# Decode attention: values of a batch issued ahead of the third part of the next batch's keys

## What is computed

```
idx = n_buf + jnp.arange(S)[:, None] - d * jnp.arange(sub_w + 1)[None, :]
s = jnp.einsum('bshd,bsjhd->bshj', q, k_all[:, idx]) * (HEAD_DIM ** -0.5)
p = jnp.exp(s - m[..., None])
acc = jnp.einsum('bshj,bsjhd->bshd', p, v_all[:, idx].astype(jnp.float32))
```

## Time and profile before

| what | value |
|---|---|
| median of 3 runs | 3102.05 us (3100.16 to 3106.0) |
| span of the profiled execution, first to last instruction | 3097.1 us |
| PE busy | 1166.9 us, 38% |
| DVE busy | 1991.4 us, 64% |
| POOL busy | 1820.1 us, 59% |
| moved by DMA | 1010.08 MB, mean 326 GB/s |

### The profile page before, as it was taken

One profiled execution on the slowest core, in us unless ns is written; L12 is line 12 of the kernel. 1 busy time (PEld: TensorE's weight loads), 2 busy tenths in 40 slices (PEclk: granted clock), 3 DMA queues, 4 the chain that ended last, 5 costly groups with the idle time before them and its releaser, 6 DMA issues.

```text
span 3097.1 us, 22146 instructions
## 1 busy us (share of the span) xinstructions
PE 1166.9 (38%) x7904; PEld 930.8 (30%) x7904; DVE 1991.4 (64%) x2265; ACT 387.5 (13%) x499; POOL 1820.1 (59%) x901
## 2 busy tenths in 40 slices
PE   7999989999896910000000003000000000000088
PEld 6889955555686910000000001000000000000077
DVE  1016441221014499898898998988888999989922
ACT  2222233433222200000000001000000000000022
POOL 4556600000453545777967778888888878873344
PEclk9999976877897955555555556555555555555599
DMA  8878869997878778889988899999999989999844
GB/s 312 312 297 312 306 189 263 253 271 210 312 298 288 288 280 330 320 340 355 384 335 328 340 396 404 401 394 385 382 387 391 409 349 401 398 390 375 328 163 170
DMA packets 161535, 1010.08 MB, mean 326 GB/s; under 512 B 18786, under 2 KB 20258, under 8 KB 71620
## 3 DMA queue, kind: packets, MB, share of 16 engines
q0 software_dynamic: 92160, 671.13, 54.5%
q1 hardware_dynamic: 69316, 338.20, 32.5%
HBM read 1002.82 MB, written 139.01 MB: 369 GB/s over the span
## 4 chain that ended last, share of the span: by engine, by line
POOL 45%; issue 42%; DVE 6%; PE 4%; DMA 2%; POOLq 1%; DVEq 0%; ACT 0%; ACTq 0%
POOL expert_rows L457 33%; POOL w_lo L438 6%; POOL pool_token L456 5%; DVE psum L1035 4%; PE psum L1137 1%; PE psum L1139 1%; PE psum L1138 1%; DMA expert_rows<-in_peer_v,block_experts 1%; DMA expert_rows<-in_peer_u,block_experts 1%; DVE expert_rows L1031 0%; POOL gate_w_lo L438 0%; DVE expert_sums L1035 0%; POOLq L455 0%; POOLq L441 0%; PE psum L1129 0%
## 5 line engine op out<-in xcount | busy, mean ns | idle before, releaser
L1031 DVE SCALAR_TENSOR_TENSOR expert_rows<-expert_rows,x_tokens 128x2048 f32<-128x2048 f32 x320 | 727.9, 2294 | 98.5 <-DMA expert_rows<-in_peer_u,block_experts 94.9
L438 POOL TENSOR_TENSOR w_lo<-w_raw,w_hi 128x2048 fp32r<-128x2048 f32 x80 | 373.8, 4673 | 702.0 <-ACT w_hi L477 702.0
L457 POOL DMA_INDIRECT expert_rows<-in_peer_u,block_experts x320 | 612.3, 1914 | 85.5 <-issue 73.3
L1035 DVE SCALAR_TENSOR_TENSOR expert_sums<-expert_rows,block_gates,expert_sums 128x2048 f32<-128x2048 f32 x256 | 603.3, 2357 | 65.8 <-DMA expert_rows<-in_peer_v,block_experts 48.2
L457 POOL DMA_INDIRECT expert_rows<-in_peer_v,block_experts x320 | 582.7, 1821 | 84.7 <-issue 73.0
L1129 PE MATMUL psum<-identity,x_tokens 128*128 128x128 f32 (+1 forms) x144 | 24.7, 356 | 1010.1 <-DVE x_tokens L880 962.0
L456 POOL TENSOR_TENSOR pool_token<-pool_token 128x1 f32<-128x1 f32 x160 | 177.8, 1111 | 301.4 <-DVE expert_rows L1031 140.1
L1129 PEld LDWEIGHTS psum<-identity,x_tokens 128*128 128x128 f32 (+1 forms) x144 | 22.6, 204 | 1012.9 <-issue 934.2
L1360 PE MATMUL psum<-identity,ple_tokens 128*128 128x128 f32 (+1 forms) x6 | 1.5, 397 | 733.8 <-DMA ple_tokens<-in_p_sample 733.8
L1360 PEld LDWEIGHTS psum<-identity,ple_tokens 128*128 128x128 f32 (+1 forms) x6 | 1.0, 210 | 734.1 <-issue 734.0
L477 ACT ACTIVATE w_hi<-w_raw 128x2048 fp32r<-128x2048 f32 x80 | 153.2, 1916 | 442.2 <-PE psum L1139 402.6
(11 more groups left out here) (234 smaller groups left out, 2315.3 us busy)
## 6 DMA issues: line engine op xcount, KB each, us to landing
out<-in_state_attn_k SPq DMA_DIRECT2D x64, 1020.0 KB, 7.4
out<-in_state_attn_v SPq DMA_DIRECT2D x64, 1020.0 KB, 15.6
w_raw<-in_w_in SPq DMA_DIRECT2D x48, 1024.0 KB, 5.3
keys_old<-in_state_attn_k SPq DMA_DIRECT2D x16, 1536.0 KB, 17.5
values_old<-in_state_attn_v SPq DMA_DIRECT2D x8, 3072.0 KB, 17.4
keys_last<-in_state_attn_k SPq DMA_DIRECT2D x8, 2048.0 KB, 13.7
values_last<-in_state_attn_v SPq DMA_DIRECT2D x8, 2048.0 KB, 21.0
w_raw<-in_w_out SPq DMA_DIRECT2D x16, 1024.0 KB, 5.0
```

Of the source, the lines that this page charges most:

```text
L438: nc.gpsimd.tensor_tensor(l_, r_, h_.bitcast(f32), ALU.subtract).then_inc(w_lo_ready, 1)
L457: pool.indirect_dma_start(ring[:, j % NSLOT, :], None, table, bass.IndirectOffsetOnAxis(idxc[:, half, j:j + 1], 0)).then_inc(g_in[j % NSLO ...
L1031: V.scalar_tensor_tensor(out=g, in0=g, scalar=1.0, in1=x, op0=ALU.mult, op1=ALU.mult, accum_out=hblk[:, c:c + 1]).then_inc(g_free, 1)
L1035: V.scalar_tensor_tensor(out=y, in0=g, scalar=ablk[:, c:c + 1], in1=y, op0=ALU.mult, op1=ALU.add).then_inc(g_free, 1)
```

## The change

SP's loop issued K0(b+1), K1(b+1), K2(b+1), then V0(b), V1(b). Now it issues K0(b+1), K1(b+1), then V0(b), V1(b), then K2(b+1). `load_k` gets two arguments that choose parts. Each transfer keeps the wait that it had. What stands ahead of the loop and behind it stays. The loop runs six times, so K2(2) to K2(7) move. No other engine's stream changes.

```
-            def load_k(b):
+            def load_k(b, first=0, past=3):
                 bb = ds(b, 1)
-                for part, last in enumerate(K_PARTS):
+                for part, last in list(enumerate(K_PARTS))[first:past]:
...
             with sp.Fori(1, NB - 1) as b:
-                load_k(b + 1)
+                load_k(b + 1, 0, 2)
                 load_v(b)
+                load_k(b + 1, 2, 3)
```

## The result

| | before | changed |
|---|---|---|
| median of 4 runs each | 3101.11 us | 3141.69 us |
| lowest to highest | 3090.87 to 3106.0 | 3131.88 to 3150.7 |
| span of the profiled execution | 3097.1 us | 3130.1 us |

The changed kernel is slower: ratio 1.0138, 95% interval 1.01 to 1.0175. The forecast was 3140 us, range 3118 to 3160. A second, longer comparison (experiment 7) gave 1.013, 1.0096 to 1.0163.

What follows compares the result with a forecast made beforehand. The decode attention was taken to go at PE's pace. 6 x 25.2 + 5 x 21.7 = 259.7 us against 221.8, so 37.9 more on 3097.1, plus 5 for the median: 3140 us, range 3118 to 3160.

Steps and rivals of the forecast that it cites:

- No gain from the part taken away: In SP's loop, K2 no longer ahead of V0 and V1 gains nothing, since PE waits for neither there.
- When V1 lands and how much longer K2 takes: In the DMA queue, V1 lands 19.9 us behind its issue and K2 5.3 later: 25.2 us (24.3 to 28.0).
- The rest of a batch: From K2's first transpose on PE to the next issue of V1: 21.7 us in each of five batches.
- The 3.3 us for slower rests: Time added in the five stretches behind K2's first transpose, for a tail at a lower clock: 3.3 us.
- When PE asks: PE asks for K2 13.5 us behind V1's issue in batch 3, 20.3 to 21.0 otherwise; waits together 34.6 us.
- The sum: From V1(1)'s issue to K2(7)'s first transpose: 259.7 us instead of 221.8, 37.9 us more.
- A lower clock: Rival: pauses delay PE's clock rise, so five tails take 26.0 us each; 59.4 us more, 3161; chance 0.10.
- Overlap: Rival: K2 fills gaps V0 leaves in the queue and lands with V1 at 19.9 us; 3109 to 3112; chance 0.07.
- The one that ends faster: Rival: K2 lands together with V1 and PE's pause is followed by full clock; 3092 to 3096; chance 0.03.

Runs made afterwards that it cites:

- experiment 7: The changed kernel run again with no edit, for a tighter interval and a second trace; ratio to the kernel before 1.013.
- experiment 1: The kernel before run again with no edit, for a second trace; ratio 0.9987.
- experiment 8: Second trace of the changed kernel with K2 issued between V0 and V1 instead of behind both; ratio to the kernel before 1.0035.
- 10: The changed kernel with the next batch's first three groups of transposes moved ahead of PE's wait for the copied output; ratio to the kernel before 1.0108.
- experiment 9: The kernel before with the next batch's first three groups of transposes moved ahead of PE's wait for the copied output; ratio 0.9953, 3088.64 us.
- experiment 4: The changed kernel with two 1020 KB cache copies moved between V1 and K2 in each of six turns; ratio to the kernel before 1.0237.

## Why the prediction was right

**No gain from the part taken away: right.** V0 and V1 landed no earlier to any use; the one wait for values stayed (7.3 us for 7.1), and no other engine's waits for them are in the list.

**When V1 lands and how much longer K2 takes: right.** I took 19.9 and 5.3 us, 25.2 together. Six batches gave 24.3 to 25.6, in sum 149.1 for 151.2. The small difference is in the first term: V1 came at 19.1 to 19.7, 19.4 on average. K2 landed 4.9 to 5.9 us behind it, 5.4 on average, so the second term was right or a little too small.

**The rest of a batch: right.** 5 x 21.7 = 108.5 us were put down; the windows that answer to the earlier trace rows sum to 108.2, from 20.8 to 22.4 us, at clocks of 0.80 to 0.87. No batch kept the full clock behind its wait. The 3.3 us for slower rests were 3.0 against the first trace, and 5.9 against that of experiment 1. K0 and K1 were through before the next V0, as said.

**When PE asks: mis-sized for batch 3.** For it I wrote 13.5 us, from the one batch that ran at full clock, and so a wait of 11.7 us and 34.6 in all. The waits were 22.3 us and the longest 4.3. There was no batch at full clock ahead of K2, in this trace or in experiment 7. It did no harm to the sum, since the sum goes from landing to landing: what isn't waited for by a quick PE is spent by a slow one. In the window it shows as longer busy time: some 10 of the 13.2 us lie ahead of K2, and some 7 of them are batch 3 at half clock instead of full. But the name was wrong, and who looked for the loss among the waits alone would have found 22.3 of 35.5 us. Experiments 8 and 10 show the wait as I had described it, 5.64 and 5.88 us with K2 landing at 19.5, and 12 to 14 us with it landing at 25, once PE is at full clock.

**The sum.** 259.7 us were forecast for the window, and 257.3 came. The span grew by 33.0 us instead of 37.9: the window gave 35.5 but began 3.5 us earlier, and 1.0 came behind it, which is within what stages vary by from run to run (the kernel before had two spans of 3097.1 and 3114.0). The median is 40.6 us above that of before. So that 3140 misses 3141.69 by only 1.7 us is in part luck: the span came 4.9 us short of the 3135.0, and the median stands 11.6 us above it, where I had added 5. Of that distance 1.8 us lie around the span (3131.88 against 3130.1 in one execution); the rest is how quick the profiled execution was among the others. What measures the working is the window, with its 2.4 us.

**The rivals.** A lower clock (0.10): the rests took 108.2 us against the 130 it asked for. Something of it may be there, since the rests of before took 105.2 and 102.3 us, but it isn't what the loss is made of. Overlap (0.07): within one queue K2 came 4.9 to 5.9 us behind V1, and even on a queue of its own it came 22.6 to 23.2 us behind V1's issue, not 19.9. The one that ends faster needed both and had neither.

## What to carry to other kernels

Issue transfers in the order in which they are asked for, and price a move by the landing: the time that the transfers ahead of it take in the queue, from the landings of the old trace, against the time at which its reader asks; the moment of issue alone costs nothing while the landing is in time. Sum such a stage from landing to landing and not wait by wait, because an engine whose clock varies turns waits into slow work and back. And look for the reader's own gaps: a transfer that seems to have room beside a slow reader has none once the reader is quick.

## What the runs showed of the hardware

I had not expected that filling a gap of at most 1.7 us a batch would change the clock so much: from 0.74 and 0.71 in the two traces of before to 0.86 in the window, and 24 to 29 us less busy time for the same matmuls. It isn't one trace's luck: over the whole execution the twelve runs of experiment 9 have clocks of 0.665 to 0.670, and the seventeen of the kernel before beside them 0.658 to 0.664. Nor that PE can be busy without a break and stay at half clock: experiment 8 has 17.00 us of 17.00 at 0.51 in one batch and 11.00 of 11.00 at 1.00 in another, in the same part of the program. What decides between the two was not settled here. Two queues shared one rate, though not evenly: V1 lost 5.9 us to a K2 that was issued later on another queue, and while both queues moved data SP's had 3.21 MB to POOL's 2.10. Bytes alone don't give the time in the queue: in the trace of before V0(4), 3072 KB over 96 partitions, landed 14.3 us behind the transfer ahead of it, and V1(4), 2048 KB over 128, 5.3 us behind V0(4). And the two 1020 KB copies of experiment 4, read and written in HBM, pushed K2's landing by 6.8 us on average (40.8 over six), 3.4 us a copy.
